# Both down projections of a two-block transformer kernel: six of eight half quarters by Strassen's seven products

## The chip, the cores and the metric

One NeuronCore of a Trainium2 chip runs the whole program. The metric is device time in microseconds (us) of that core, the median of three executions. The engines are TensorE (PE), VectorE (DVE), ScalarE (ACT), GpSimd (POOL) and SyncE (SP, which here only starts transfers).

## The reference

Two transformer blocks on 512 tokens of 1024 features, in float32. Each has mixers (convolution, sparse attention, cross attention; then a chunked linear recurrence and a latent attention) and ends in a feed forward. Only the feed forwards matter here:

```python
hf = _rmsnorm(h, norm_ffn_g[l]) @ w_ff1[l]            # 512x1024 @ 1024x4096
h = h + jnp.square(jax.nn.relu(hf)) @ w_ff2[l]        # 512x4096 @ 4096x1024
...
y = jnp.square(jax.nn.relu(m @ w_up[l])) @ w_down[l]
x = x + rmsnorm(y, norm_post_mlp[l])
```

## The kernel before, in words

Every float32 operand is split in two float32r parts, a rounded "hi" and the remainder "lo", and a product is three matmuls, hi by hi, lo by hi and hi by lo (L511 to L515). Activations lie feature by feature: 128 features on the partitions, 512 tokens along the row. A weight chunk is 1024 rows by 128 columns, 128x1024 in the memory, and gives one output of 128x512 with 8 x 3 = 24 matmuls (L524).

**The weight ring.** All chunks come in the order of their use through a ring of four slots. SP starts the transfer of chunk c when chunk c-4 is used up (L386 to L391). ACT rounds it to w_hi (L1218), POOL writes the remainder w_lo in place of the raw weights (L410), PE waits for w_lo_done. ACT keeps three chunks ahead.

**A feed forward** is four groups of 16 chunks. Eight "up" chunks (L829) give eight blocks of the hidden layer: DVE takes relu and the norm's scale (L2146), ACT squares (L1494) and rounds (L1496), DVE writes the remainder b_lo (L2149). Then eight "down" chunks multiply these eight blocks, and DVE adds each output to res (first block) or ffy (second), L2157. So 64 ups and 64 downs in all. The first block's feed forward is FF1 in the code, the second's FF2. A group works on a quarter of the 4096 hidden features; a half quarter is four up chunks and 512 hidden features.

**Around them.** Beside the first group of FF1 DVE computes the angles of the rotary embedding (`rotary`, L2186 to L2206, steps that wait for each other) and ACT their sines. FF2's first three chunks are computed in two halves of tokens while DVE, POOL and ACT still normalize the mixer's output (L1130 to L1161; post_scale L2510, post_split L2520, post_tree L2528 on DVE; post_add L485 on POOL; post_row on ACT). PE sums squares for a norm with a matmul by ones (`stat`), ACT takes the root (L1232), DVE the reciprocal (L1767, L2571).

Each engine executes its instructions in the order in which its block of the program issues them, and semaphores are the only order between engines. An engine that waits holds back all that is written behind the wait.

Of the kernel before, what the change touches and what calls it, by code (L numbers as in the profile page):

```python
# [20 lines left out]
ALU = mybir.AluOpType  # L21
# [29 lines left out]
FF_GROUPS = 4  # L51
# [10 lines left out]
          ("GL", 3), ("AO", 8), ("CO", 8), ("MX", 8), ("QX", 4), ("OX", 4), ("FF1", 64), ("CQ", 2), ("CKV", 1),  # L62
          ("KR", 1), ("QK", 4), ("UQ", 2), ("UKV", 1), ("OA", 1), ("VM", 4), ("OM", 3), ("WO", 8), ("FF2", 64)]
CH = {}
_n = 0
for _name, _count in STAGES:
# [5 lines left out]
        ("GL", 3), ("AO", 8), ("CO", 8), ("MX", 8), ("QX", 4), ("OX", 8), ("FF1", 64), ("CQ", 2), ("CKV", 1),  # L72
        ("KR", 1), ("QK", 4), ("UQ", 8), ("UKV", 8), ("OA", 1), ("VM", 4), ("OM", 3), ("WO", 11), ("FF2", 68)]
# [55 lines left out]
angles centred cn_hi_done cn_ready cn_scaled conv_done convact_ready cq_squared f_hi f_ready f_sq floors_done  # L129
gains_ready gate_step gated gates_done gates_late gates_turned gcols_done hg_hi hg_ready ki_split kr_moved  # L130
kv_keys_done kv_odd kv_values_done late_landed ln_added ln_hi ln_inv ln_root ln_scaled ln_silu ln_squared ln_sum
logits_ready mean2 mem_added mem_scaled mem_squared mix_added mix_hi mix_ready ml_conv ml_decay ml_den ml_diag
ml_floor ml_gated ml_hi ml_inv ml_mrow ml_ones ml_out ml_ready ml_root ml_s ml_sT ml_saved ml_scaled ml_sq
ml_turned ml_var norm2 o_gated o_hi o_ready o_scaled o_turned ox_first pT_copied pT_ready p_inv p_ready p_scaled
pad_zeroed post_added post_first post_scaled post_summed pv_done q_moved q_roped q_zeroed qi_split qk_pad
qk_rows_zeroed qk_silu relu_ready res_sq res_sqg rope_done rope_q rope_step row_step rows_done rstd_ready
rt_cols rt_done rt_turned s_masked s_ready scales_ready score_added sines spread_done squares
squares_added ssq_added ssqg_added start_hi start_ready start_scaled stat_ready stat_root tap_done topk_done
topk_step uq_out vm_rows wi_copied wi_turned x2_done x2_gained y_pool y_scaled y_written half_done half_rooted half_sums part_sq part_ssq qk_tanh post_tree post_sq first_w first_x first_hi first_lo
# [28 lines left out]
def program(nc, stream, xT, memT, cols_in, consts_in, pos_in, out):  # L168
    with ExitStack() as ctx:
# [80 lines left out]
        ff_f = at("ff_f", [P, 2, T], TMP0 + 4096)  # L250
# [68 lines left out]
        x_landed = [sem(f"x_landed{i}") for i in range(RING)]  # L319
# [43 lines left out]
        def up_bank(s, g, o0, j):  # L363

            if s == 1 and g == 0 and j in (4, 5):
                return j + 2
            return (o0 + j) % RING
# [6 lines left out]
        def _(sp):  # L374
# [11 lines left out]
            with sp.Fori(1, CHUNKS // RING) as i:  # L386
                for j in range(RING):
                    sp.wait_ge(chunk_done, RING * i + j - (RING - 1))
                    sp.dma_start(w_raw[:, j, :],
                                 stream[bass.ds(RING * i + j, 1), :, :].rearrange("o p n -> (o p) n")  # L390
                                 ).then_inc(raw_landed[j], 16)  # L391
            vector_adds = [j for j in range(KB) if j not in POOL_ADDS]
# [12 lines left out]
        def _(pool):  # L405
# [6 lines left out]

            last = CH["FF2"] // RING
# [7 lines left out]
            pool.wait_ge(sems["first_hi"], 1)  # L421
            first_remainder(0, sems["first_lo"])
# [3 lines left out]
            with pool.Fori(1, CH["CQ"] // RING) as i:  # L426
                for j in range(RING):
                    remainder(RING * i + j, j)
            pool.wait_ge(sems["pv_done"], 4 * MLA_G)
# [65 lines left out]
            with pool.Fori(last + 1, CHUNKS // RING) as i:  # L495
                for j in range(RING):
                    remainder(RING * i + j, j)
# [9 lines left out]
        def _(pe):  # L507
# [147 lines left out]
            def first_values():  # L655
                for kk in range(2):
                    w = slice(kk * T, (kk + 1) * T)
                    pe.wait_ge(w_hi_done if kk else sems["first_hi"], 1)
# [3 lines left out]
                for kk in range(2):  # L662
                    w = slice(kk * T, (kk + 1) * T)
                    pe.wait_ge(w_lo_done if kk else sems["first_lo"], 1)
# [2125 lines left out]
```

## Time and profile before

| | |
|---|---|
| median of three executions | 1583.17 us (1582.39 to 1584.31) |
| span of the profiled execution, first to last instruction | 1579.8 us |
| PE busy | 1545.0 us, 98% of the span, 7370 matmuls |
| POOL, DVE, ACT busy | 653.6, 838.6, 652.4 us |
| share of the chain that ended last | PE 90%, DVE 4%, ACT 2%, POOL 1% |

No time of its own is listed for the profiled execution beside its span; the median of the executions lies 3.4 us above that span. A busy share is the share of the span in which an engine has an instruction under way. Matmuls overlap, so their pace is read from the distance of their starts, not from their durations.

### The profile page before, as it was taken

How to read it: one execution, taken by the hardware profiler on the slowest of the kernel's cores; microseconds unless marked ns; L12 is line 12 of the kernel's file. 1: busy time of each engine (PE TensorE's matmuls, PEld its weight loads, DVE VectorE, ACT ScalarE, POOL GpSimd, SP SyncE). 2: the span in 40 equal slices, each digit the busy share in tenths (PEclk: the TensorE clock that was granted, in tenths of full speed). 3: DMA queues.
4: the chain of work that ended last, by engine and by line, in shares of the span. 5: the costliest groups of instructions: out<-in, count | busy, mean ns of one | idle time of the engine just before them, and what ended most of it. 6: DMA issues, size and time to landing. Idle time of an engine off the chain costs nothing.

```text
span 1579.8 us, 21097 instructions
## 1 busy us (share of the span) xinstructions
PE 1545.0 (98%) x7370; PEld 1278.8 (81%) x7370; DVE 838.6 (53%) x1486; ACT 652.4 (41%) x1066; POOL 653.6 (41%) x299
## 2 busy tenths in 40 slices
PE   8999999999999999999999999999999999999997
PEld 6888888787788877888888888777778888888887
DVE  5689999877785446442112124877645612111125
ACT  6553333444552445523233244455754514232331
POOL 3454444323344433444444445442524544444442
PEclk9999999999999999999999999999999999999999
DMA  5332333222333322323333333221112333333332
GB/s 208 102 121 94 94 101 98 67 67 67 107 95 102 96 67 67 101 93 99 101 93 93 104 96 94 83 71 61 41 49 73 96 104 93 94 98 102 94 93 81
DMA packets 41412, 144.57 MB, mean 92 GB/s; under 512 B 4596, under 2 KB 6772, under 8 KB 41080
## 3 DMA queue, kind: packets, MB, share of 16 engines
q1 hardware_dynamic: 40320, 139.94, 28.7%
q10 hardware_dynamic: 1016, 3.62, 0.7%
q8 instruction: 48, 0.79, 0.2%
q14 instruction: 28, 0.23, 0.1%
HBM read 141.43 MB, written 2.11 MB: 91 GB/s over the span
## 4 chain that ended last, share of the span: by engine, by line
PE 90%; DVE 4%; issue 3%; ACT 2%; POOL 1%; DMA 0%; DVEq 0%; SPq 0%; POOLq 0%; ACTq 0%
PE bank L509 88%; PE bank L619 1%; POOL w_lo L410 1%; POOL res L485 1%; DVE cq_rstd L1767 0%; PE bank L1014 0%; DVE bias L1913 0%; ACT w_hi L1218 0%; DMA x_raw<-in_xT 0%; DMA w_raw<-in_stream 0%; ACT kT L1392 0%; DVE cn_lo L2261 0%; DVE gt L2284 0%; DVE ffy L2600 0%; ACT probs L1251 0%
## 5 line engine op out<-in xcount | busy, mean ns | idle before, releaser
L410 POOL TENSOR_TENSOR w_lo<-w_raw,w_hi 128x1024 fp32r<-128x1024 f32 x250 | 602.6, 2411 | 849.6 <-ACT w_hi L1218 849.2
L1218 ACT CAST w_hi<-w_raw 128x1024 fp32r<-128x1024 f32 x255 | 267.4, 1049 | 499.2 <-DMA w_raw<-in_stream 499.2
L509 PE MATMUL bank<-a_hi,w_hi 128*128 128x512 f32 (+1 forms) x1120 | 445.0, 397 | 3.1 <-DVE a_lo L2520 1.8
L509 PE MATMUL bank<-a_hi,w_lo 128*128 128x512 f32 (+1 forms) x1120 | 431.5, 385 | 0.0
L509 PE MATMUL bank<-a_lo,w_hi 128*128 128x512 f32 (+1 forms) x1120 | 431.2, 385 | 0.0
L509 PEld LDWEIGHTS bank<-a_hi,w_hi 128*128 128x128 f32 x1120 | 210.5, 188 | 50.9 <-issue 4.2
L509 PEld LDWEIGHTS bank<-a_lo,w_hi 128*128 128x128 f32 x1120 | 210.6, 188 | 45.6 <-issue 3.6
L509 PEld LDWEIGHTS bank<-a_hi,w_lo 128*128 128x128 f32 x1120 | 210.4, 188 | 42.3
L509 PE MATMUL bank<-b_hi,w_hi 128*128 128x512 f32 (+1 forms) x640 | 244.3, 382 | 0.0
L509 PE MATMUL bank<-b_hi,w_lo 128*128 128x512 f32 (+1 forms) x640 | 242.3, 379 | 0.0
L509 PE MATMUL bank<-b_lo,w_hi 128*128 128x512 f32 (+1 forms) x640 | 242.2, 378 | 0.0
L509 PEld LDWEIGHTS bank<-b_hi,w_hi 128*128 128x128 f32 x640 | 120.4, 188 | 22.8 <-issue 0.2
L509 PEld LDWEIGHTS bank<-b_lo,w_hi 128*128 128x128 f32 x640 | 120.4, 188 | 22.5 <-issue 0.2
L509 PEld LDWEIGHTS bank<-b_hi,w_lo 128*128 128x128 f32 x640 | 120.4, 188 | 22.5
L2146 DVE SCALAR_TENSOR_TENSOR ff_t<-bank,rstd 128x512 f32<-128x512 f32 x64 | 44.1, 689 | 148.5 <-PE bank L509 148.4
L2149 DVE TENSOR_TENSOR b_lo<-ff_f,b_hi 128x512 fp32r<-128x512 f32 x64 | 47.9, 748 | 86.8 <-ACT b_hi L1496 86.8
L1977 DVE SCALAR_TENSOR_TENSOR bank<-conv_in,cols,bank 128x512 f32<-128x512 f32 x114 | 82.3, 749 | 1.6
L2157 DVE TENSOR_TENSOR res<-bank,res 128x512 f32<-128x512 f32 x32 | 22.1, 691 | 109.0 <-PE bank L509 109.0
L1956 DVE SCALAR_TENSOR_TENSOR bank<-conv_in,cols,bank 128x512 f32<-128x512 f32 x116 | 76.5, 745 | 0.0
L1494 ACT ACTIVATE ff_f<-ff_t 128x512 f32<-128x512 f32 x64 | 40.5, 632 | 85.5 <-DVE ff_t L2146 85.5
L2157 DVE TENSOR_TENSOR ffy<-bank,ffy 128x512 f32<-128x512 f32 x20 | 13.8, 691 | 84.3 <-PE bank L509 84.3
L1260 ACT COPY probsT<-bank 128x256 f32<-128x256 f32 (+3 forms) x48 | 19.6, 409 | 58.0 <-PE bank L619 58.0
(355 smaller groups left out, 1961.3 us busy)
## 6 DMA issues: line engine op xcount, KB each, us to landing
w_raw<-in_stream SPq DMA_DIRECT2D x255, 512.0 KB, 3.5
res<-in_xT ACTq DMA_DIRECT2D x1, 2048.0 KB, 8.0
out_y<-y_out SPq DMA_DIRECT2D x16, 128.0 KB, 1.8
x_raw<-in_xT SPq DMA_DIRECT2D x3, 512.0 KB, 8.3
mem_raw<-in_memT SPq DMA_DIRECT2D x1, 1024.0 KB, 11.9
mrow<-m_rows ACTq DMA_DIRECT2D x4, 256.0 KB, 3.2
w_raw<-in_stream SPq DMA_DIRECT2D x2, 256.0 KB, 3.6
x_raw<-in_xT SPq DMA_DIRECT2D x2, 256.0 KB, 4.2
```

Source lines behind the costliest of these rows:

```text
L410: nc.gpsimd.tensor_tensor(w_lo[:, j, :], w_raw[:, j, :], w_hi[:, j, :].bitcast(F32), ALU.subtract).then_inc(w_lo_done, 1)
L485: nc.gpsimd.tensor_tensor(res[:, j, t], res[:, j, t], mixed[:, j, t], ALU.add).then_inc(sems["post_added"], 1)
L509: return nc.tensor.matmul(o, l, r, start=start, stop=stop)
L619: m = nc.tensor.transpose(turned_bank(U)[:, r], probs[:, U % 2, r], ident)
L1218: A.copy(w_hi[:, slot, :], w_raw[:, slot, :]).then_inc(w_hi_done, 1)
L1260: A.copy(probsT[:, U % 2, r], turned_bank(U)[:, r]).then_inc(sems["pT_copied"], 1)
L1494: A.activation(ff_f[:, j % 2, :], ff_t[:, j % 2, :], ACT.Square).then_inc(sems["f_sq"], 1)
L1956: V.scalar_tensor_tensor(out=blk(conv_io, e, 0, T) if last else acc, in0=u, scalar=w, in1=acc, op0=ALU.mult, op1=ALU.add).then_inc(sems["c ...
L1977: m = V.scalar_tensor_tensor(out=out, in0=u, scalar=w, in1=acc if start is None else start, op0=ALU.mult, op1=ALU.add)
L2146: V.scalar_tensor_tensor(out=ff_t[:, j % 2, :], in0=bank, scalar=0.0, in1=rstd[:, :], op0=ALU.max, op1=ALU.mult).then_inc(evac_dve, 1)
L2149: V.tensor_tensor(b_lo[:, j, :], ff_f[:, j % 2, :], b_hi[:, j, :].bitcast(F32), ALU.subtract).then_inc(sems["f_ready"], 1)
L2157: V.tensor_tensor(dst[:, i, :], bank, dst[:, i, :], ALU.add).then_inc(evac_dve, 1)
```

## The change

Hidden block and down weights of a half quarter are 512 tokens by 512 hidden features and 512 by 1024. Split into 2x2 blocks (tokens in halves, hidden blocks by even and odd, outputs in halves), the product takes eight block products, or seven by Strassen's method (in Winograd's form) with sums of blocks on both sides. Six half quarters of each feed forward go that way; the last quarter (8 ups, 8 downs) stays as it was. The hidden block is now the stationary operand, so the results lie token by token (ytok) and are turned back on PE in the last quarter, where DVE scales them by rstd squared (r2) and adds them.

Weights: the four blocks of a half quarter (L11, L21, L22, L12, each 128x1024) come by four transfers outside the ring into dn_raw. DVE makes four sums of them, ACT rounds seven (`top`), POOL writes seven remainders in place (`rest`). FF1 and FF2 have 40 ring chunks each in place of 64, and 24 blocks beside them.

```diff
+            def product(s, g, n, x, banks):
+                q = HALVES * s + g
+                pe.wait_ge(sems["apart_lo"], APART + PRODUCTS * q + n + 1)
+                for h in range(2):
...
+                    for p in range(2):
...
+                        mm(o, xh, wh, p == 0, False)
+                        mm(o, xh, wl, False, False)
+                        m = mm(o, xl, wh, False, p == 1)
+                    m.then_inc(sems["dn_done"], 1)
+            def ff_down(s, g):
+                last, evac = 4 * g + 2, evac_before(s, g)
...
+                pe.wait_ge(sems["b_ready"], b_at(s, last, 1))
+                product(s, g, M1, E1, (4, 5))
...
+                pe.wait_ge(sems["b_ready"], b_at(s, last, 2))
+                product(s, g, M5, T1, (6, 7))
...
+                product(s, g, M7, T3, (0, 1))
+                product(s, g, M6, T2, (2, 3))
+                pe.wait_ge(sems["dn_evac"], evac + 2 * (M7 + 1))
+                product(s, g, M4, T4, (0, 1))
...
+                product(s, g, M2, O1, (4, 5))
+                product(s, g, M3, O2, (6, 7))
+            def turn_block(s, i):
...
+                for tb in range(TB):
+                    m = nc.tensor.transpose(ps[4 + i % RING][:, tb * P:(tb + 1) * P],
+                                            ytok[:, tb, i * P:(i + 1) * P], ident)
```

POOL, in order of its queue (`remainder` is the ring's w_lo):

```diff
+            def rest(s, g, names=BY_ORDER):      # L11 S1 S3 S2 L22 L12 S4
+                for name in names:
+                    pool.wait_ge(sems["apart_hi"], APART + PRODUCTS * q + n + 1)
+                    if name in ("L11", "S1"):
+                        pool.wait_ge(sems["dn_sum"], 4 * q + 3)
+                    elif name == "L22":
+                        pool.wait_ge(sems["dn_sum"], 4 * q + 2)
+                    elif name in ("S2", "L12"):
+                        pool.wait_ge(sems["dn_sum"], 4 * q + 4)
+                    nc.gpsimd.tensor_tensor(dn_rest[:, n, :], dn_raw[:, n, :], dn_top[n].bitcast(F32), ALU.subtract
...
+            for g in range(HALVES):
+                rest(0, g)
+                for c in range(CH["FF1"] + 4 * (g + 1), CH["FF1"] + 4 * (g + 2)):
+                    remainder(c, c % RING)
...
+            remainder(CH["FF2"] + 4, 0)
+            rest(1, 0, ("L11",))
+            remainder(CH["FF2"] + 5, 1)
+            rest(1, 0, BY_ORDER[1:])
+            remainder(CH["FF2"] + 6, 2)
+            remainder(CH["FF2"] + 7, 3)
+            rest(1, 1)
+            for g in range(2, HALVES):
+                for c in range(CH["FF2"] + 4 * g, CH["FF2"] + 4 * g + 4):
+                    remainder(c, c % RING)
+                rest(1, g)
```

ACT, one half quarter:

```diff
+            def ff_half(s, g):
+                j = 4 * g
+                square_up(s, j)
+                even_casts(s, j)          # E1, T1: 256 columns each
+                top(s, g, "S2", "L22")
+                square_up(s, j + 1)
+                odd_casts(s, j + 1)       # T3: 256; T2 and T4: 512; O1 and O2: 512
+                top(s, g, "L12", "S4")
+                square_up(s, j + 2)
+                even_casts(s, j + 2)
+                square_up(s, j + 3)
+                odd_casts(s, j + 3)
+                round_to(ff_chunk_at(s, j + 7) - AHEAD)
...
+            top(0, 0, "L11", "S1", "S3")
+            root(3, rstd[:, :], STAT, 1.0 / D)
+            ff_half(0, 0)
+            for g in range(1, HALVES):
+                top(0, g, "L11", "S1", "S3")
+                ff_half(0, g)
```

DVE, one half quarter (even_block: one sum of 256 columns; even_lo: two remainders of 256; odd_block: three sums of 256, remainders of 256, 512 and 512; left_sum: 1024 columns; take_products: fourteen results of 128x512 from PSUM):

```diff
+                evict_up(s, j)
+                even_block(s, j)
+                even_lo(s, j)
+                left_sum(s, g, "S4")
+                evict_up(s, j + 1)
+                odd_block(s, j + 1)
+                evict_up(s, j + 2)
+                even_block(s, j + 2)
+                even_lo(s, j + 2)
+                evict_up(s, j + 3)
+                odd_block(s, j + 3)
+                take_products(s, g)
...
+            for g in range(1, HALVES):
+                left_sum(0, g, "S3")
+                left_sum(0, g, "S1")
+                left_sum(0, g, "S2")
+                ff_half(0, g)
+            ff_whole(0)                   # seven sums of 128x1024, then r2
+            ff_last(0, res, last_ff1, rotary)
```

In FF2 the first two half quarters are ordered by hand (DVE after post_tree):

```diff
+            evict_up(1, 0)
+            evict_up(1, 1)
+            even_block(1, 0)
+            even_lo(1, 0)
+            evict_up(1, 2)
+            evict_up(1, 3)
+            left_sum(1, 0, "S3")
+            left_sum(1, 0, "S1")
+            even_block(1, 2)
+            even_lo(1, 2)
+            odd_block(1, 1)
+            left_sum(1, 0, "S2")
+            odd_block(1, 3)
+            left_sum(1, 0, "S4")
+            evict_up(1, 4)
+            evict_up(1, 5)
```

ACT's order there is round_to(FF2+1), square_up 0 and 1, even_casts 0, round_to(FF2+2), square_up 2 and 3, even_casts 2, root(9), top S1 and S3, odd_casts 1, top S2, odd_casts 3, top L22, L12, S4. PE computes chunks 3, 4 and 5, then ff_down(1, 0), chunks 6 and 7, ff_down(1, 1). The rotary work of DVE and ACT moves from FF1's first downs to its last ups (`if j == 4`, `if 4 < j < 7`, counted from 0 in the last quarter).

## Rows read from the trace of the kernel before

**Rows 1.** The page, sections 1 and 4: busy time, and the chain by engine and line

```profile
PE 1545.0 (98%) x7370; PEld 1278.8 (81%) x7370; DVE 838.6 (53%) x1486; ACT 652.4 (41%) x1066; POOL 653.6 (41%) x299
...
PE bank L509 88%; PE bank L619 1%; POOL w_lo L410 1%; POOL res L485 1%; DVE cq_rstd L1767 0%; PE bank L1014 0%; DVE bias L1913 0%; ACT w_hi L1218 0%; DMA x_raw<-in_xT 0%; DMA w_raw<-in_stream 0%; ACT kT L1392 0%; DVE cn_lo L2261 0%; DVE gt L2284 0%; DVE ffy L2600 0%; ACT probs L1251 0%
```

**Rows 2.** DVE in order of time, a down of FF1: start, us, instruction, idle before

```profile
709.84 0.69 DVE L2157 TENSOR_TENSOR res<-bank,res 128x512 f32<-128x512 f32 x1 [4.75 <-PE bank L509]
```

**Rows 3.** PE in order of time: four transposes between 512-column matmuls

```profile
999.73 0.60 PE L866 MATMUL bank<-consts,ssq 128*128 128x128 f32 x4
1000.08 0.47 PE L509 MATMUL bank<-a_hi,w_hi 128*128 128x512 f32 x1
1000.40 0.39 PE L509 MATMUL bank<-a_lo,w_hi 128*128 128x512 f32 x1
```

**Rows 4.** By source line: duration ns min/median/max, first and last start, forms

```profile
L410 POOL TENSOR_TENSOR w_lo<-w_raw,w_hi x250: 2358/2400/2854, 20.8 to 1549.7; 128x1024 fp32r<-128x1024 f32 x125
L1218 ACT CAST w_hi<-w_raw x255: 1029/1050/1066, 8.6 to 1548.5; 128x1024 fp32r<-128x1024 f32 x128
L1494 ACT ACTIVATE ff_f<-ff_t x64: 632/632/635, 644.6 to 1523.7; 128x512 f32<-128x512 f32 x64
L1842 DVE TENSOR_TENSOR w_lo<-w_raw,w_hi x5: 1217/1226/1566, 9.7 to 1217.0; 128x1024 fp32r<-128x1024 f32 x5
L2149 DVE TENSOR_TENSOR b_lo<-ff_f,b_hi x64: 691/692/1306, 645.9 to 1525.0; 128x512 fp32r<-128x512 f32 x64
L2154 DVE COPY ffy<-bank x8: 690/692/692, 1267.3 to 1305.4; 128x512 f32<-128x512 f32 x8
```

**Rows 5.** DVE and ACT in order of time: instructions of 256 columns

```profile
1196.90 0.43 DVE L2494 TENSOR_TENSOR ssq<-ssq,sq 128x256 f32<-128x256 f32 x1 [0.48 <-ACT sq L1691]
...
1196.45 0.42 ACT L1691 ACTIVATE sq<-mixed 128x256 f32<-128x256 f32 x1 [1.97 <-DVE mixed L2485]
```

**Rows 6.** POOL, then DVE, in order of time from 1253 to 1259 us

```profile
1253.29 2.41 POOL L410 TENSOR_TENSOR w_lo<-w_raw,w_hi 128x1024 fp32r<-128x1024 f32 x1 [8.79 <-ACT w_hi L1218]
1255.94 2.57 POOL L410 TENSOR_TENSOR w_lo<-w_raw,w_hi 128x1024 fp32r<-128x1024 f32 x1 [0.24 <-ACT w_hi L1218]
...
1254.94 1.31 DVE L2149 TENSOR_TENSOR b_lo<-ff_f,b_hi 128x512 fp32r<-128x512 f32 x1 [1.35 <-ACT b_hi L1496]
```

**Rows 7.** The same two engines at 20 us (DVE's four merged)

```profile
20.75 2.73 POOL L410 TENSOR_TENSOR w_lo<-w_raw,w_hi 128x1024 fp32r<-128x1024 f32 x1 [12.92 <-ACT w_hi L1218]
23.70 2.59 POOL L410 TENSOR_TENSOR w_lo<-w_raw,w_hi 128x1024 fp32r<-128x1024 f32 x1 [0.21 <-ACT w_hi L1218]
...
19.75 7.09 DVE L1831 TENSOR_TENSOR x_sq<-x_sq 128x512 f32<-128x512 f32 x4
```

**Rows 8.** The page, section 6: transfers of a weight chunk, KB, us to landing

```profile
w_raw<-in_stream SPq DMA_DIRECT2D x255, 512.0 KB, 3.5
```

**Rows 9.** Start of FF1: its first matmul on PE, DVE's last sum before it

```profile
627.13 0.39 PE L509 MATMUL bank<-a_hi,w_hi 128*128 128x512 f32 x1
...
634.37 0.68 DVE L2089 TENSOR_TENSOR ssq<-ssq,sq 128x512 f32<-128x512 f32 x1
```

**Rows 10.** Start of FF2: PE's chunk 3, DVE's last tree, ACT's cast of chunk 4

```profile
1232.87 0.40 PE L509 MATMUL bank<-a_hi,w_hi 128*128 128x512 f32 x1
...
1230.06 4.85 DVE L2528 TENSOR_TENSOR mixed<-mixed 128x1024 f32<-128x1024 f32 x6
...
1236.13 1.05 ACT L1218 CAST w_hi<-w_raw 128x1024 fp32r<-128x1024 f32 x1 [6.20 <-DMA w_raw<-in_stream]
```

**Rows 11.** PE's last dense matmul; window: busy by engine, granted clock, DMA, GB/s

```profile
1568.76 0.28 PE L509 MATMUL bank<-b_hi,w_lo 128*128 128x256 f32 x1
...
1570.00:1575.00 5.00, 1.54 (x10) 1.26 (x10) 2.99 (x10) 0.26 (x1) 1.56 (x2) 0.78 0.04 13
```

**Rows 12.** PE's first matmuls, eight of 512 columns

```profile
5.82 3.88 PE L509 MATMUL bank<-w_hi,xu_hi 128*128 128x512 f32 x8 [5.82 <-ACT xu_hi L1297]
9.54 2.01 PE L509 MATMUL bank<-w_lo,xu_hi 128*128 128x512 f32 x8
```

More of the change, by code:

```diff
@@ L50, with done_before, evac_before, added_at @@
 MLA_V = 64
-FF_GROUPS = 4
+HALVES = 6
+UPS = 4 * HALVES
+BY_ORDER = ("L11", "S1", "S3", "S2", "L22", "L12", "S4")
+SLOT = {name: n for n, name in enumerate(BY_ORDER)}
+LEFT = ("L11", "L21", "L22", "L12")
+SLOT["L21"] = SLOT["S1"]
+M1, M5, M7, M6, M4, M2, M3 = range(7)
+E1, O1, O2, T1, T3, T2, T4 = range(7)
+PRODUCTS = 7
+PARTS_DONE = 2 * PRODUCTS
+WHOLE_STEPS = 7
+def done_before(s, g):
+    return (PARTS_DONE * HALVES + KB) * s + PARTS_DONE * g
+def evac_before(s, g):
+    return (PARTS_DONE * HALVES + WHOLE_STEPS + 1 + 2 * KB) * s + PARTS_DONE * g
+def added_at(s, i):
+    return evac_before(s, HALVES) + WHOLE_STEPS + 1 + (2 - s) * (i + 1)
+def evens_first(s, g):
+    return s == 1 and g < 2
+def b_before(s, g):
+    return (10 * HALVES + KB) * s + 10 * g
+def b_at(s, j, n):
+    g, p = j // 4, j // 2 % 2
+    if evens_first(s, g):
+        return b_before(s, g) + (2 * p + n if n <= 2 else 2 + 3 * p + n)
+    return b_before(s, g) + 5 * p + n
+def sum_at(s, j, n):
+    g, p = j // 4, j // 2 % 2
+    if evens_first(s, g):
+        return 8 * (HALVES * s + g) + (p + n if n == 1 else 1 + 3 * p + n)
+    return 8 * (HALVES * s + g) + 4 * p + n
 RING = 4
@@ L318, in program @@
         mem_landed = sem("mem_landed")
[L319 removed]
+        x_landed = [sem(f"x{i}_and_{name}_landed") for i, name in enumerate(LEFT)]
+        dn_landed, LANDED_X, APART = x_landed, 16, 1
         x_again = sem("x_landed_again")
@@ L854, in norm_ffn, with ff_up @@
-            def norm_ffn():
-                stat(3, STAT, [(sems["ssq_added"], 2 * KB, ssq[:, :])])
-            feed_forward("FF1", 0, 1, norm_ffn, 1)
+            def ff_up(s, j, ks=range(KB), ready=None, base=0):
+                c, o = ff_chunk_at(s, j), ff_out_at(s, j)
+                g = j // 4
+                if g > 0 and ks[0] == 0 and up_bank(s, j) < RING:
+                    pe.wait_ge(sems["dn_evac"], evac_before(s, min(g, HALVES) - 1) + 2 * (M4 + 1))
+                chunk(c, c % RING, o if up_bank(s, j) < RING else None, up_bank(s, j), a_hi, a_lo, T, ready, base, ks=ks)
@@ new lines, in ff_last @@
+            def ff_last(s, downs):
+                for j in range(KB):
+                    ff_up(s, UPS + j)
+                    if 2 <= j < 6:
+                        turn_block(s, 2 * j - 4)
+                        turn_block(s, 2 * j - 3)
+                for j in range(UPS + KB, UPS + KB + downs):
+                    c, o = ff_chunk_at(s, j), ff_out_at(s, j)
+                    chunk(c, c % RING, o, o % RING, b_hi, b_lo, T, sems["b_ready"] if j == UPS + KB else None, b_before(s, HALVES))
@@ new lines, in take @@
+            def take(s, g, n, dst, banks):
+                for h in range(2):
+                    dve.wait_ge(sems["dn_done"], done_before(s, g) + 2 * n + h + 1)
+                    bank = ps[banks[h]][:, :]
+                    if g == 0:
+                        V.tensor_copy(dst[h], bank).then_inc(sems["dn_evac"], 1)
+                    else:
+                        dve.wait_ge(sems["dn_evac"], evac_before(s, g - 1) + 2 * n + h + 1)
+                        V.tensor_tensor(dst[h], bank, dst[h], ALU.add).then_inc(sems["dn_evac"], 1)
```

558 lines of the change are left out of this document (417 added, 141 removed).

## The prediction

> **What bounds the kernel now.** I read the page first. PE is busy for 1545.0 of 1579.8 us, and its matmuls are 88% of the chain that ended last; no other engine passes 53% [rows 1]. Next comes the order of time inside a feed forward: DVE takes one output of 24 matmuls in 0.69 us after an idle 4.75 us that PE ends [rows 2]. So a chunk is 5.44 us of PE, a matmul of 512 columns 0.227 us, and each matmul taken from PE is worth that as long as nothing else comes late. Then I looked at what the other engines' instructions cost alone and beside each other, since the change loads DVE and POOL.
>
> **What goes.** A half quarter now has 4 ups and 4 downs, 8 x 24 matmuls. The seven products have 12 each: 84 in place of 96. Twelve halves save 144 x 0.227 = 32.6 us.
>
> **Transposes.** 16 blocks of four. Four transposes move the second matmul behind them from 0.227 to 0.67 us after their start [rows 3], 0.44 us a block: 16 x 0.44 = 7.0 us. The Trainium skill, "TensorE: Matmul & The Clock Gate", Part 4: PE-mode transpose, has about 275 ns for one transpose in a kernel; by it the 64 would cost 17.6 us and the sum would be 10.6 us higher. The trace has such durations too, but shows them overlapping, so I go by the starts.
>
> **Prices of the added work.** DVE with 1024 columns 1.22 us, with 512 columns 0.69 (from PSUM too), ACT's cast of 1024 columns 1.05 and square 0.63, POOL's remainder 2.40 [rows 4]; 256 columns 0.43 on DVE, 0.42 on ACT [rows 5]. A relu without the norm's scale has no row; I take the 0.69 of a PSUM read (it could be 0.43, the row of half its columns, or 0.75).
>
> **What decides: DVE and POOL hold each other up.** A b_lo of 0.69 us took 1.31 where POOL's remainder ran: POOL ended at 1255.70, b_lo 0.55 us later, at 1256.25. POOL's next, which had started at 1255.94, ended 2.26 us after that [rows 6]. At 20 us DVE had four instructions to do in a row and needed 7.09 us for them, 2.4 us of which is their own; working back from the ends, POOL got in behind the second and again behind the third [rows 7]. So two-input DVE work in SBUF and POOL's remainders exclude each other, and when both queue up they take turns: DVE pays the rest of a POOL instruction (up to 2.3 us) for each of its own. Before, POOL ran one remainder per 5.44 us, and this hid. Now a half quarter has 7 + 4 remainders (26.4 us) and 22 such DVE instructions.
>
> **A half in the steady state**, from the start u of its ups (the last product of the half before ends). DVE takes that product until u+0.8, then S3, S1, S2 at 1.24 each: u+4.5. Only now may POOL start L11. From here, with s = time since S2:
> - POOL L11, S1, S3, and between them DVE's three short ones (t1, E1 lo, T1 lo; 0.3 us each when admitted): s = 8.1. DVE's S4 sum: 9.3.
> - POOL's S2 runs (2.4) while DVE evicts the second block and ACT squares it: 11.7. T3 sum 0.3, POOL's L22 2.26, T2 sum 0.3, T4 sum 0.45: 15.0.
> - ACT casts T2/T4 and O1/O2 (1.1), then tops L12 and S4 (1.9), and only then squares the third block (0.63): s = 18.6. POOL's L12 has begun at 17.2 and ends at 19.6; t1 of the third block 19.9; POOL's S4 has the turn, 22.1; E1 lo 22.4.
> M1 waits for that E1 lo: u+26.97. The four ups end at u+21.76. **PE waits 5.2 us.** All later products are covered: T3 lo is ready 3 us after M1 begins, M7 needs it after 5.4, and DVE's takes keep up with 2.72 us a product. The half takes 21.76+5.2+19.04 = 46.0 us where it took 43.5.
> Transfers land in 3.5 us [rows 8]; L22's slot is free 5.4 us before u, L12's 2.7 before, so they are no wait, nor are SP's ring transfers queued behind them.
>
> **First half of FF1.** Ups begin at 627.13, DVE is free at 635.0 [rows 9]. S3, S1, S2 with one POOL remainder between end at 640.8; ACT's root and its table load follow two tops, so the first square is at about 643.6. The same chain gives M1 at 663.8; the ups end at 649.6: 14.2 us.
> **FF1's last quarter.** ff_whole, seven sums of 1.22 us, delays the evictions but four banks cover it. DVE then has evict, remainder, two turned blocks (3.6 to 4.3 us) per up, and at the sixth and seventh up also seven rotary steps, 3.9 us bare and about 6 with POOL's turns. It runs about 8 us late, and the first down lacks its last block for 5.5 us. The cover these steps had, DVE's idle 4.75 us per down, is gone.
> **Start of FF2.** Chunk 3 begins at 1232.87, DVE's tree ends at 1234.9, ACT casts chunk 4 from 1236.13 [rows 10]. DVE reaches the S2 sum only behind two odd or even blocks that wait for ACT (squares, root, tops S1 and S3, casts): at 1252.8. POOL's rest of L11 waits for it, and **behind that on POOL stands chunk 5's remainder**: ready at 1257.7, PE came at 1244.5. 13.2 us, and 1.0 more for bank 7 before M5. Second half: S2 sum at 1295.8, L11 at 1298.3 against 1294.2 (4.1), then 0.4 for T3 and 2.3 for rest S2, whose sum S4 came late by two turns: 6.8. Third half: POOL is still at four ring remainders when DVE wants its sums, S2 4.2 us later than in the steady state: 9.4.
>
> **The sum.** Waits of FF1: 14.2 + 5 x 5.2 + 5.5 = 45.7. Of FF2: 13.2+1.0 + 6.8 + 9.4 + 3 x 5.2 = 46.0. Together 91.7 - 32.6 + 7.0 = +66.1 us.
> **The clock** comes on top. The dense matmuls ended at 1568.9 us; in the window 1570 to 1575 the mean grant is 0.78, so 2.4 GHz was granted for 2.8 us of it, to 1572.8, and 1.2 GHz then: 3.9 us after, with a few small matmuls between [rows 11]. At the start eight matmuls took 3.72 us where eight take 1.8 at full clock [rows 12]: 1.9 us for a fall. Three long waits surely pay it (5.7); of the nine of 5.2 to 5.5 us, between none and all (17.1): half, 8.5, since one fall beside small matmuls can't say more. +14. The skill's same page, "Why this matters for your kernels", advises to leave no idle gaps between bursts of matmuls, since they bring the low clock back; by it all twelve waits pay, and the time would be 1672. The trace has no such gap between dense matmuls.
> Against the profiled span of 1579.8 that gives 1660; the median is 3.4 above that span: **1663 us**, bounds 1649 (no falls) to 1680 (all falls and longer waits); evictions at the ends of their range move each half by under 0.3 us.
>
> **Rivals.**
> - *DVE keeps the turn in a run of short sums.* For: each of its instructions waits in the queue ready. Against: rows 7. T1 lo and T2 sum each save 2.3 us, a steady half waits 0.7. Waits: 8 x 0.7, 9.7 at FF1, 11 + 5 + 5 in FF2, 5 rotary: 41, clock 4: 1583.2-25.6+45 = 1603.
> - *The exclusion doesn't reach these instructions* (smaller, or hidden in gaps). Then every steady wait is gone; what stays is chunk 5's place on POOL's queue (11), the second half's late sum (4), the rotary (4), one fall (2): 1583.2-25.6+21 = 1579, faster. Its place is the wait of M1; it decides once POOL's seven rests need under 17 us from S2 with DVE's work between (22.4 by my walk).
> - *PE stays the bound everywhere*, by the same and with ACT's and POOL's start-up work landing early: 1583.2-25.6 = 1557.6. Against it: POOL can't have chunk 5 before DVE's S2 sum. That the matmuls don't go can't be: the count is fixed in the code.
>
> **Chances.** Forecast (1640 to 1690) 0.73, first rival 0.12, second 0.09, third 0.06. Slower by over 0.2% (about what a measurement of this kernel can tell): 0.73+0.12 = 0.85, less 0.01; the second lies at -0.3%: 0.07 faster, 0.02 same; with the third and a hundredth more for same: faster 0.13, same 0.03, slower 0.84. Range: the forecast's case and nearly all of the first rival, 1600 to 1690.
>
> **What would show it.** Right: PE waits before M1 of each half, ended by DVE's f7_lo (E1), about 5 us each; before chunk 5 of FF2 a wait ended by POOL, over 10 us; DVE sums of 256 columns with a mean well over 1 us; POOL near two thirds busy in the halves; starts of products 0.227 us apart; PE clock below 1 in slices. Wrong: DVE's 256-column sums at 0.43 us, or halves of 41 us, or waits ended by transfers.

## The result, and the profile after

The changed kernel takes **1678.15 us** (1674.69 to 1679.59), the kernel before, run beside it, 1583.74: a ratio of 1.059, 95% interval 1.058 to 1.061, 94.4 us slower. The forecast was 1663 us. The spans of the profiled executions differ by 98.0 us (1677.8 against 1579.8); the sums below go by these two.

The page of the changed kernel, its sections 1, 2 (the clock's line) and 5:

```profile
span 1677.8 us, 20806 instructions
PE 1553.3 (93%) x7290; PEld 1279.1 (76%) x7290; DVE 1196.9 (71%) x1862; ACT 704.2 (42%) x1174; POOL 745.6 (44%) x335
...
PEclk9999999999999998999999999999999898999998
...
L655 PE MATMUL bank<-dn_first,f_hi 128*128 128x512 f32 x192 | 84.8, 442 | 71.2 <-issue 66.1
```

Against [rows 1]: 80 instructions fewer on PE (144 matmuls less, 64 transposes more), yet PE is busy 8 us longer, because part of them ran at the lower clock. DVE gained 358 us, POOL 92. PE's idle time grew from 34.8 to 124.5 us. The last line says where: of 71.2 us before matmuls with `dn_first` (rounded weights, L11 for M1), 66.1 are marked "issue", which means that the view found no releaser. The line alone doesn't say what PE waited for. The waits of PE, grouped (us in total, times, longest):

```profile
PE bank L655 <- issue: 66.3, 11, 13.2
PE bank L655 <- POOL w_lo L524: 10.8, 2, 9.8
...
PE bank L655 <- DVE b_lo L2578: 6.0, 2, 4.9
PE bank L655 <- POOL dn_rest L538: 5.2, 2, 4.2
```

and PE in order of time: the first matmul of M1 in FF1's first four halves, then FF2's start, where the first line is chunk 5's and the two others M1's in the second and third halves:

```profile
663.40 0.77 PE L655 MATMUL bank<-dn_first,f_hi 128*128 128x512 f32 x1 [13.16 <-issue]
715.13 0.77 PE L655 MATMUL bank<-dn_first,f_hi 128*128 128x512 f32 x1 [8.43 <-issue]
763.23 0.77 PE L655 MATMUL bank<-dn_first,f_hi 128*128 128x512 f32 x1 [5.06 <-issue]
811.21 0.77 PE L655 MATMUL bank<-dn_first,f_hi 128*128 128x512 f32 x1 [5.05 <-issue]
...
1310.51 0.79 PE L655 MATMUL bank<-a_hi,w_hi 128*128 128x512 f32 x1 [9.75 <-POOL w_lo L524]
...
1353.26 0.47 PE L655 MATMUL bank<-dn_first,f_hi 128*128 128x512 f32 x1 [4.21 <-POOL dn_rest L538]
...
1406.26 0.77 PE L655 MATMUL bank<-dn_first,f_hi 128*128 128x512 f32 x1 [9.09 <-issue]
```

Two more of FF1 and three of FF2 are like the third and fourth. For what M1 waits DVE's order of time tells, from the half's first block on:

```profile
791.27 0.48 DVE L2460 TENSOR_TENSOR comb<-ff_f 128x256 f32<-128x256 f32 x1 [0.70 <-ACT ff_f L1703]
791.71 2.58 DVE L2466 TENSOR_TENSOR f_lo<-ff_f,f_hi 128x256 fp32r<-128x256 f32 x1
794.22 2.61 DVE L2469 TENSOR_TENSOR f_lo<-comb,f_hi 128x256 fp32r<-128x256 f32 x1
...
807.43 1.20 DVE L2460 TENSOR_TENSOR comb<-ff_f 128x256 f32<-128x256 f32 x1 [1.05 <-ACT ff_f L1703]
808.55 2.56 DVE L2466 TENSOR_TENSOR f_lo<-ff_f,f_hi 128x256 fp32r<-128x256 f32 x1
```

and POOL's beside it (the first line is three rests merged):

```profile
789.07 7.48 POOL L538 TENSOR_TENSOR dn_rest<-dn_raw,dn_first 128x1024 fp32r<-128x1024 f32 x3 [11.38 <-DVE dn_raw L2438]
798.11 2.40 POOL L538 TENSOR_TENSOR dn_rest<-dn_raw,dn_first 128x1024 fp32r<-128x1024 f32 x1 [1.57 <-DVE dn_raw L2444]
800.47 2.58 POOL L538 TENSOR_TENSOR dn_rest<-dn_raw,dn_second 128x1024 fp32r<-128x1024 f32 x1
806.00 4.83 POOL L538 TENSOR_TENSOR dn_rest<-dn_raw,dn_second 128x1024 fp32r<-128x1024 f32 x2 [2.95 <-ACT dn_second L1697]
```

E1's remainder of the half's third block (L2466) ends at 811.11 and M1 begins at 811.21: that is the "issue". An operation of 256 columns, 0.43 us alone [rows 5], takes 2.56 to 2.61 us here where a rest of POOL began just before it, and 1.20 where the rest was already half done. Between two such operations one rest passes, never two. The view by source line has the spread (ns min/median/max; first and last start):

```profile
L2466 DVE TENSOR_TENSOR f_lo<-ff_f,f_hi x24: 414/2564/2628, 646.2 to 1549.0; 128x256 fp32r<-128x256 f32 x24
```

Set beside POOL's timeline, 20 of the 24 take 2.56 to 2.63 us, and a rest had begun 0.24 to 0.28 us before each of them. The other four, of FF2's first two halves, take 0.41 or 0.42, and no rest runs beside them.

### The profile page after: what moved, and what is told of

Same layout as the page of the kernel before. It is cut to its first block and busy times, and to the rows that moved or that the text cites. A ratio compares the mean times of both kernels' runs of the same rounds, so it can differ in the third digit from the quotient of the medians.

```text
span 1677.8 us, 20806 instructions
## 1 busy us (share of the span) xinstructions
PE 1553.3 (93%) x7290; PEld 1279.1 (76%) x7290; DVE 1196.9 (71%) x1862; ACT 704.2 (42%) x1174; POOL 745.6 (44%) x335
## 5 line engine op out<-in xcount | busy, mean ns | idle before, releaser
L524 POOL TENSOR_TENSOR w_lo<-w_raw,w_hi 128x1024 fp32r<-128x1024 f32 x202 | 488.8, 2429 | 668.6 <-ACT w_hi L1427 668.5
L655 PEld LDWEIGHTS bank<-a_hi,w_lo 128*128 128x128 f32 x1120 | 211.1, 188 | 42.7
L538 POOL TENSOR_TENSOR dn_rest<-dn_raw,dn_first 128x1024 fp32r<-128x1024 f32 x48 | 118.2, 2483 | 153.2 <-DVE dn_raw L2438 131.2
L655 PE MATMUL bank<-dn_first,f_hi 128*128 128x512 f32 x192 | 84.8, 442 | 71.2 <-issue 66.1
L655 PE MATMUL bank<-dn_rest,f_hi 128*128 128x512 f32 x336 | 139.5, 415 | 0.0
L655 PE MATMUL bank<-b_hi,w_hi 128*128 128x512 f32 (+1 forms) x256 | 95.9, 374 | 6.0 <-DVE b_lo L2578 6.0
L538 POOL TENSOR_TENSOR dn_rest<-dn_raw,dn_second 128x1024 fp32r<-128x1024 f32 x36 | 88.3, 2470 | 29.5 <-ACT dn_second L1697 29.5
L655 PE MATMUL bank<-b_hi,w_lo 128*128 128x512 f32 (+1 forms) x256 | 93.4, 365 | 0.0
L655 PE MATMUL bank<-b_lo,w_hi 128*128 128x512 f32 (+1 forms) x256 | 93.3, 365 | 0.0
L655 PE MATMUL bank<-dn_first,f_lo 128*128 128x512 f32 x192 | 82.6, 430 | 0.0
L655 PEld LDWEIGHTS bank<-dn_rest,f_hi 128*128 128x128 f32 x336 | 68.3, 203 | 14.5
```

The lines of the kernel that those rows point to most:

```text
L524: nc.gpsimd.tensor_tensor(w_lo[:, j, :], w_raw[:, j, :], w_hi[:, j, :].bitcast(F32), ALU.subtract).then_inc(w_lo_done, 1)
L538: nc.gpsimd.tensor_tensor(dn_rest[:, n, :], dn_raw[:, n, :], dn_top[n].bitcast(F32), ALU.subtract).then_inc(sems["apart_lo"], 1)
L655: return nc.tensor.matmul(o, l, r, start=start, stop=stop)
```

## The experiments

My theory after this reading: PE's waits before M1 come from **turns** that DVE and POOL take at a shared access to SBUF (the on-chip memory that both read), two waits in FF2's start from the **order of POOL's queue**, two at FF1's end from the **rotary steps**, and each wait of some 5 us costs about 2.3 us more by **TensorE's clock**. Ratios are against the kernel before on the same chip, with 95% intervals; line numbers shift by one to seven between kernels.

### POOL's rests read nothing

```diff
-                    nc.gpsimd.tensor_tensor(dn_rest[:, n, :], dn_raw[:, n, :], dn_top[n].bitcast(F32), ALU.subtract
-                                            ).then_inc(sems["apart_lo"], 1)
+                    nc.gpsimd.memset(dn_rest[:, n, :].bitcast(F32), 0.0).then_inc(sems["blank"], 1)
+                    pool.wait_ge(sems["blank"], PRODUCTS * q + BY_ORDER.index(name) + 1)
+                    nc.gpsimd.memset(dn_rest[:, n, :].bitcast(F32), 0.0).then_inc(sems["apart_lo"], 1)
```

> POOL's seven remainders of a half quarter are left out: in their place two memsets of 1024 columns each write zeros there (so the hi-by-lo share of the products is missing). POOL then still takes time for each of the seven, but reads nothing from SBUF. Theory (DVE and POOL exclude each other and take turns): the waits of PE before the first product M1, 5.06 us in the steady state, fall under 1 us, DVE's E1 remainders (median 2.56 us now) go back to 0.43, the first half of FF1 waits under 4 us where it waited 13.2; with the clock's falls gone too the time is 1590 to 1610. The wait before FF2's chunk 5 stays at 7 us or more, since it is an order on POOL's queue. Rival (the order of ACT's and DVE's own queues sets M1, POOL's port doesn't matter): waits before M1 stay at 4 us or more and the time is over 1660.

Measured: **1593.72 us**, ratio 1.006 (1.004 to 1.009), as the theory had it. The same line of DVE, and the waits that PE has left:

```profile
L2467 DVE TENSOR_TENSOR f_lo<-ff_f,f_hi x24: 412/426/426, 646.1 to 1467.0; 128x256 fp32r<-128x256 f32 x24
```

```profile
PE bank L656 <- POOL w_lo L524: 10.6, 2, 9.6
...
PE bank L656 <- DVE b_lo L2579: 5.3, 2, 4.9
PE bank L656 <- POOL dn_rest L540: 3.8, 1, 3.8
PE bank L656 <- issue: 3.7, 1, 3.7
```

All 24 are at 0.41 to 0.43 us, and no steady half waits for M1, while DVE's queue, ACT's and the matmuls are as in the changed kernel. The edit also makes a rest shorter (1.91 us for two memsets of 0.956 where it was 2.36), so by this run alone some of the gain could be POOL's; the run with ACT's casts in another order, below, keeps all of the reads and settles that. What stays, the 9.6 of chunk 5, the 4.9 of FF1's first down, the 3.8 of FF2's second half and the 3.7 of FF1's first, doesn't need POOL's reads.

### PE kept busy before M1

```diff
+                    for _ in range(24):
+                        mm(ps[4][:, :], a_hi[:, 0, 0:P], a_hi[:, 0, :])
                 pe.wait_ge(sems["b_ready"], b_at(s, last, 1))
                 product(s, g, M1, E1, (4, 5))
```

> 24 matmuls of 512 columns, whose result is overwritten, stand before M1 of each half but the first of each feed forward, so PE works through 5.44 us of the wait. Theory (each wait also costs about 2.2 us of low clock behind it): M1 comes 0.4 us later than before, but the halves take 46.3 us where they take 47.8 to 48.1, the granted clock stays at full in them, and the time is about 1660. Rival (the falls cost nothing that counts, the 2 us a half are something else): 1680 to 1684.

Measured: **1663.84 us**, 1.051 (1.048 to 1.053). M1 to M1 in steady halves takes 46.26 us (763.99 to 810.23, to 856.50) where it took 47.98 and 47.88. The waits are as long as before, only filled with matmuls of no use (5.45 us for 5.06), and 46.26 is 40.8 and 5.45: nothing of the clock is left in such a half, where it had been 2.0 to 2.1 us. The time is 14 us shorter, as expected.

### The order of ACT's last two casts, and POOL's last three rests held back

First the casts alone:

```diff
                 odd_casts(s, j + 1)
-                top(s, g, "L12", "S4")
                 square_up(s, j + 2)
                 even_casts(s, j + 2)
+                top(s, g, "L12", "S4")
```

> One move on ACT's queue: the tops of L12 and S4 come after the casts of the third block instead of before its square. All work stays. Theory: the square comes only 0.4 us earlier, but POOL has no remainder ready to take the turn when t1 and E1 lo of the third block come, so M1's wait falls from 5.06 to about 1.9 us, the eight steady ones together by 25 us, and the clock's falls mostly go: 1637. Rival (ACT's order alone): each wait 0.4 to 1.5 us shorter, 1665 to 1675. Rival (only the number of instructions on the port counts): no change.

Measured: **1642.9 us**, 1.038 (1.035 to 1.040). The waits of 5.06 before M1 became 1.87 to 1.88, and the two of 8.43 and 9.09 became 5.26 and 5.94; in two halves a new one of 1.3 stands before M7. The third block of a half, DVE and then POOL:

```profile
841.89 0.42 DVE L2460 TENSOR_TENSOR comb<-ff_f 128x256 f32<-128x256 f32 x1 [0.70 <-ACT ff_f L1703]
842.33 0.43 DVE L2466 TENSOR_TENSOR f_lo<-ff_f,f_hi 128x256 fp32r<-128x256 f32 x1
```

```profile
843.78 4.93 POOL L538 TENSOR_TENSOR dn_rest<-dn_raw,dn_second 128x1024 fp32r<-128x1024 f32 x2 [5.91 <-ACT dn_second L1697]
```

This is the plainest proof of the turns, since all of the work and all of POOL's reads are there. ACT's square starts only 0.36 us earlier behind DVE's relu than in the changed kernel (0.72 us after the relu's start, 1.08 before). The other 2.9 us are DVE's two short operations, 1.20 and 2.56 us when two rests stood beside them [807.43 and 808.55 above], 0.42 and 0.43 now that POOL's rests come behind them. Together they are, to 0.1 us, what M1's wait lost. The rival of ACT's order alone (1665 to 1675 us) is out.

Then POOL's rests of L22, L12 and S4 behind T3's remainder of the fourth block as well:

```diff
+            def rest_held(s, g):
+                rest(s, g, BY_ORDER[:4])
+                pool.wait_ge(sems["b_ready"], b_at(s, 4 * g + 2, 3))
+                rest(s, g, BY_ORDER[4:])
```

> As the ACT order alone, and POOL also holds its remainders of L22, L12 and S4 back until T3 lo of the fourth block is done, so that they run while DVE reads PSUM. All work stays. Theory: steady waits before M1 under 1 us, no wait before M4, M2, M3, POOL's ring remainders end about 2 us into the next ups; time 1605 to 1620. If POOL's work and not the turns was the limit, new waits before M4 to M3 or before the next ups take their place and the time stays over 1650.

Measured: **1636.11 us**, 1.033 (1.031 to 1.035), a miss: 16 us above what was expected at most. The steady halves no longer wait for M1, but before M4, 2.2 us each:

```profile
761.68 0.80 PE L660 MATMUL bank<-dn_second,f_hi 128*128 128x512 f32 x1 [2.21 <-DVE ytok L2505]
```

because a part of the turns had been moved, onto the remainders of 512 columns behind the hold (DVE, then POOL):

```profile
797.34 2.69 DVE L2491 TENSOR_TENSOR f_lo<-comb,f_hi 128x512 fp32r<-128x512 f32 x1 [0.35 <-ACT f_hi L1724]
799.96 2.90 DVE L2494 TENSOR_TENSOR f_lo<-ff_f,f_hi 128x512 fp32r<-128x512 f32 x1
```

```profile
797.07 8.03 POOL L538 TENSOR_TENSOR dn_rest<-dn_raw,dn_second 128x1024 fp32r<-128x1024 f32 x3 [9.32 <-DVE f_lo L2488]
```

DVE then takes the products' results 4 us late, and M4 waits for M7's bank. I had not looked at who needs DVE next behind the hold. Even so a half is shorter, 43.3 us where no fall of the clock follows the wait, against 44.5 with the casts' order alone.

### The two orders at the quarters' ends

Chunk 5's remainder ahead of the rest of L11:

```diff
             remainder(CH["FF2"] + 4, 0)
-            rest(1, 0, ("L11",))
             remainder(CH["FF2"] + 5, 1)
+            rest(1, 0, ("L11",))
```

> One line moved: on POOL the remainder of FF2's chunk 5 now stands ahead of the half's rest of L11. Theory (chunk 5 waits only because its remainder is queued behind L11's, which waits for DVE's S2 sum): the 9.75 us before chunk 5 go, M1 of that half waits instead for L11's chain, some 2 to 4 us; with the clock of one wait that comes to 1668 to 1672 us. Rival (chunk 5 is late for ACT's cast or its transfer): no change from 1678.

Measured: **1676.33 us**, 1.059 (1.057 to 1.061), no different from the changed kernel: a miss. Chunk 5 no longer waits, so its place on the queue was the cause of that wait (the 0.9 us before chunk 4 stay), but two others, before M1 and before M5, stand where one stood:

```profile
1310.18 0.76 PE L655 MATMUL bank<-dn_first,f_hi 128*128 128x512 f32 x1 [3.63 <-POOL dn_rest L538]
1318.95 0.80 PE L655 MATMUL bank<-dn_first,f_hi 128*128 128x512 f32 x1 [4.19 <-DVE ff_t L2452]
```

7.8 us in place of 9.75, and each with a fall of the clock. The second is M5, whose bank DVE has yet to empty of the up before (the 1.0 us that the prediction has for it, now in the open). All of this stands behind one DVE chain, the S2 sum and then the odd block, with POOL's turns in it.

The rotary steps back beside the downs (DVE's part of the edit; ACT's two sines move with them):

```diff
-                if j == 4:
+                if j == KB:
...
-                if 4 < j < 7:
-                    dst, turn_off, off = ((sinT, 0.0, 0.0), (cosT, 0.25, float(np.pi / 2)))[j - 5]
-                    n = 2 + 6 * (j - 5)
+                if KB < j < KB + 3:
+                    dst, turn_off, off = ((sinT, 0.0, 0.0), (cosT, 0.25, float(np.pi / 2)))[j - KB - 1]
+                    n = 2 + 6 * (j - KB - 1)
```

> The rotary steps on DVE and ACT's two sines go back from FF1's ups (the fifth to seventh) to its third to fifth downs from last. Theory: DVE is no longer behind in the last quarter, the waits of 1.16 and 4.88 us before the last two blocks of FF1's first down go: 1668 to 1672 us. Rival (DVE is late there for its turned blocks alone, two of them per up): most of the 6 us stays, 1675 or more.

Measured: **1672.96 us** (two runs, 1668.16 and 1677.76), 1.057 (1.053 to 1.061). Both waits of FF1's first down (1.16 and 4.88) are gone, which the rival did not have; a new one of 2.20 us stands ahead of the mixer, ended by DVE's a_lo. The two times are too far apart to size the gain (mean granted clock 0.974 in the shorter, 0.966 in the other, whose trace this is).

### All of these together, with the hold lengthened

The hold of `rest_held` at `b_at(s, 4 * g + 2, 5)`, so behind the fourth block's last remainder.

> e4's edit (ACT's tops of L12 and S4 behind the third block's casts, POOL's rests of L22, L12 and S4 held back), with the hold lengthened from the fourth block's E1 remainder to its O remainders, so that none of DVE's remainders of the half meets POOL's last three rests; and with the edits of e5 and e6. Theory of turns: both e4's gains stay and its 2.2 us before M4 go too, as well as chunk 5's and the rotary's wait; what is left are the first halves' waits (7.6, 3.1 us): 1595 to 1605 us. Rival (the 2.2 us before M4 come from DVE's work alone): about 1620.

Measured: **1616.79 us**, 1.022 (1.020 to 1.024), 12 us above what the theory had at most. The time is near the rival's 1620, but not for its reason: the waits before M4 are gone, so DVE's work alone didn't make them. 1.7 to 1.8 us before M1 are back in most steady halves, which take 42.7 to 42.9 us. One more hold, so that DVE's first two remainders meet no rest:

```diff
-                rest(s, g, BY_ORDER[:4])
+                rest(s, g, BY_ORDER[:1])
+                pool.wait_ge(sems["b_ready"], b_at(s, 4 * g, 2))
+                rest(s, g, BY_ORDER[1:4])
```

> e8's kernel with one more hold: POOL rests L11, then waits for T1's remainder of the half's first block, and only then rests S1 and S3. Theory of turns: DVE's two remainders there (2.6 us each in e8, 0.43 alone) no longer pay, DVE is 3 to 4 us earlier, and the last 1.7 to 1.8 us before M1 go, half of the first halves' too: 1597 to 1607 us. Rival (the shared access is full, 39.7 us of the 40.8 of a half: 11 remainders of 2.36 and DVE's 13.7, so what one hold gives the next wait takes): 1612 to 1620.

Measured: **1615.12 us**, 1.020 (1.018 to 1.022): the rival's number, and not clearly less than without the second hold. DVE in order of time:

```profile
775.82 0.41 DVE L2473 TENSOR_TENSOR f_lo<-ff_f,f_hi 128x256 fp32r<-128x256 f32 x1
776.37 0.42 DVE L2476 TENSOR_TENSOR f_lo<-comb,f_hi 128x256 fp32r<-128x256 f32 x1
...
780.40 2.62 DVE L2486 TENSOR_TENSOR comb<-ff_f,comb 128x256 f32<-128x256 f32 x1
783.05 2.51 DVE L2488 TENSOR_TENSOR comb<-ff_f,comb 128x256 f32<-128x256 f32 x1
```

The two remainders are short, as the hold wants, and the two sums of the next block are long in their place. M1 waits 1.63. By an estimate from these durations the access is nearly full: in a half POOL needs 11 x 2.38 = 26.2 us of it, DVE four sums of 1.22, fourteen operations of 256 columns at 0.42 and four of 512 at 0.69, 13.5 together; that is 39.7 of the 40.8 us in which PE does the half's matmuls (4 x 5.44 + 84 x 0.227). The orders did give back most of the turns' price: a steady half takes 42.7 us here, 47.9 in the changed kernel. The last 1.9 us I put down to the full access; that no order could win them too is not shown.

### Both: no reads, and the two orders

> e1's edit (each POOL rest replaced by two memsets, which read nothing; the products' share of high part by rest of the second matrix is left out) with the edits of e5 and e6. Theory: the removed matmuls are worth their 25.6 us when nothing else is late; what is left are short waits in the first halves and before M1 in the second half: 1565 to 1578 us, below the kernel before. Rival (the clock or a hidden cost of the products takes it anyway): no less than 1583.

Measured: **1584.35 us** (1577.75 to 1585.3), ratio 1.000 (0.9985 to 1.0013): no difference, where 5 to 18 us of gain were expected. The steady halves take 40.8 us (696.61 to 737.41 to 778.21), the full gain of the removed matmuls, and little else is late.

Against the profiled 1579.8: -32.6 and +7.0, 15.0 us of waits that the kernel before has not (3.59, 0.98, 3.19, 3.79, 2.18, 1.25), together -10.6. The span is 1582.6, so 13.4 more. The granted clock was low six times before the tail, in a window of one of them (us, PE busy, clock, DMA share, GB/s):

```profile
1048.00:1051.00 3.00, 3.00 (x9) 0.50 0.02 5
```

Six falls at 2.3 us would be 13.8. Added up from the granted clock itself it is less: PE works 22.5 us at half clock before the tail, which costs 11.2. Two of the six falls lie in the mixer, which the change does not touch, and where the kernel before has nearly the same short waits (1.38 us for ogate, 1.82 here) and no fall; a third lies in FF2's first chunk, behind the wait of 1.25. So the rival that the clock takes it had a part of the truth. The ten executions bear it out: three took 1577.8 to 1579.2 us, at a mean granted clock of 0.994, the other seven 1583.7 to 1585.3, at 0.989 or 0.990.

### What a gap costs by itself

The kernel **before**, with twelve gaps in dense matmuls; the second run has GAP = 2:

```diff
+GAPS = (9, 12, 14)
+GAP = 7
...
+                        if j in GAPS:
+                            pe.wait_ge(sems["pad_zeroed"], gap_at(s, g, j, GAP))
                         ff_chunk(g, j, sems["f_ready"] if j == KB else None, g * KB + 32 * s)
...
+                        if not isinstance(g, int) and j + 1 in GAPS:
+                            for n in range(GAP):
+                                if n > 0:
+                                    dve.wait_ge(sems["pad_zeroed"], gap_at(s, g, j + 1, n))
+                                V.memset(ps[6][:, :], 0.0).then_inc(sems["pad_zeroed"], 1)
```

> The kernel before (not the changed one), with twelve gaps put into PE's dense matmuls in the middle quarters of the feed forwards: in front of the second, fifth and seventh down PE waits until DVE has taken the down before and filled an unused PSUM bank seven times, one after the other. Nothing else is late by it. It measures what a gap of about 5 us costs besides its own length. As the mis-sized term of the changed kernel's sum has it (35 us of clock in place of 14, with 14 waits of 4 to 13 us), a gap costs 2 to 3 us more than it lasts: with gaps of w us the time is 1583 + 12 x (w + 2.5), 1673 at w = 5. If falls of the clock are not it, and the 21 us are another loss of the changed kernel (its matmuls, its transposes), the time is 1583 + 12 x w to 12 x (w + 1).

> The same with two fillings in place of seven, gaps of 1.5 to 2.5 us. The changed kernel's waits of 1 us mostly show no fall of the granted clock and those of 3 us do, so I expect some of the twelve to fall: 1583 + 12 x w plus 0 to 20 us. If every gap pays alike, it is 12 x 2.5 = 30 us on top of the gaps.

Measured: **1684.65 us** with the long gaps, **1626.64** with the short ones. PE in order of time around one long gap, and the granted clock in windows there:

```profile
771.00 0.79 PE L517 MATMUL bank<-b_hi,w_hi 128*128 128x512 f32 x1 [5.63 <-DVE bank L2172]
771.58 0.63 PE L517 MATMUL bank<-b_lo,w_hi 128*128 128x512 f32 x1
772.01 0.63 PE L517 MATMUL bank<-b_hi,w_lo 128*128 128x512 f32 x1
...
776.09 0.40 PE L517 MATMUL bank<-b_hi,w_hi 128*128 128x512 f32 x1
```

```profile
768.50:769.00 0.50, 0.00 (x0) 1.00 0.06 25
769.00:770.00 1.00, 0.00 (x0) 0.50 0.00 0
...
775.00:776.00 1.00, 1.00 (x4) 0.58 0.00 0
```

The clock goes to 1.2 GHz (0.50) inside the gap, and the next eleven matmuls start 0.43 us apart in place of 0.227. The long gaps sum to 68.3 us; the kernel is 102.3 us longer, so 34.0 us are beside their length, one more fall in the mixer included: **2.6 us for each of the 13 falls**. In one group of downs, with three gaps (759.76 to 828.11, less the 43.52 without gaps and the 16.89 of the gaps), it is 2.65. All twelve show the fall. Of the twelve short ones (2.3 to 2.45 us, 27.8 in all) six do. The execution with the trace (1624.47 us) is 42.1 us longer than the kernel before, 14.3 beside the gaps, or 2.0 for each of seven falls, one of them again in the mixer; in a stretch of three short gaps with one fall the trace has 2.4. The other execution took 1628.81 us at a lower mean clock (0.988 against 0.990) and has no trace.

## Why the prediction was right

The likeliest case came true at its place and in its sign. Point by point, with the numbers of the changed kernel:

- **What goes, and the transposes:** 80 instructions fewer, as counted. Ups with two blocks of transposes beside them begin 6.34 us apart (951.06 to 957.40), 0.90 more than 5.44: 0.45 a block, where 0.44 was taken. The durations' reading, 17.6 us for the 64, is refuted.

```profile
951.06 0.48 PE L655 MATMUL bank<-a_hi,w_hi 128*128 128x512 f32 x1
957.40 0.47 PE L655 MATMUL bank<-a_hi,w_hi 128*128 128x512 f32 x1
```

- **Steady halves:** 5.06 us before M1, seven times, 5.2 forecast for eight. The walk through the three queues, turn by turn, was right to 0.15 us, and the run in which POOL reads nothing and the one with the casts' order show its cause. A relu without the norm's scale took 0.68 us, where 0.69 was taken.
- **First half of FF1:** 13.16 for 14.2. **Its second half:** 8.43 for 5.2, missed. The step that failed is that this half was taken as a steady one: ahead of its sums DVE has the reciprocal of the norm's root to do, 3.34 us, which is the whole difference, and which the prediction has no term for. POOL had ended its ring remainders at 677.85 us and stood idle for 15.1:

```profile
685.59 3.34 DVE L2050 RECIPROCAL rstd<-rstd 128x512 f32<-128x512 f32 x1
```

- **FF2's third half:** 9.09 for 9.4. POOL's four ring remainders (1371.12 to 1381.58) met two of DVE's sums, 3.27 and 3.24 us for 1.22, as the prediction had it:

```profile
1376.06 3.27 DVE L2429 TENSOR_TENSOR dn_raw<-dn_raw 128x1024 f32<-128x1024 f32 x1
```

- **FF1's first down:** 1.16 and 4.88, 6.04 for 5.5. The late rotary steps are the cause: put back, both waits are gone.
- **Chunk 5:** 9.75 for 13.2, with 1.05 before chunk 4 that was not forecast. POOL's queue shows the order that made it, the rest of L11 idle until DVE's S2 sum and chunk 5's remainder behind it:

```profile
1305.58 2.40 POOL L538 TENSOR_TENSOR dn_rest<-dn_raw,dn_first 128x1024 fp32r<-128x1024 f32 x1 [11.51 <-DVE dn_raw L2438]
1307.94 2.52 POOL L524 TENSOR_TENSOR w_lo<-w_raw,w_hi 128x1024 fp32r<-128x1024 f32 x1
```

- **Second half of FF2:** 4.21 and 0.95, 5.2 for 6.8. The 4.2 us stand in every run that does all of the work but the one whose filler matmuls cover a part; no experiment was made for them.
- **The waits together** are 88.1 us, 91.7 forecast.
- **The clock is the term that was mis-sized.** 98.0 + 32.6 - 7.0 - 88.1 leaves 35.5 us, where 14 was taken. The step that failed is "half of nine" at 1.9 us a fall, and with it the list of twelve waits: all 13 waits over 4 us brought the clock down (the 13th is the 4.21 of FF2's second half, which the list leaves out), and so did all twelve gaps of 5.6 us put into the kernel before; and two falls lie in the mixer, which had no term. Added up from the granted clock, PE works 62.2 us at half clock before the tail, which costs 31.1 us, about 2.1 for each of the 15 falls. So most of the miss is their number, 15 where seven or eight were priced. Some 4 us of the 35.5 are not the clock's by this sum; the tail behind the last product is 0.9 us longer, and for the rest I have no row. The Trainium skill ("TensorE: Matmul & The Clock Gate", Why this matters for your kernels), by whose rule all waits pay and which the prediction priced at 1672 us, agrees with these traces in that: none of the 13 was without a fall. The 1672 us were still low, since they leave out the three falls more and price each at the 1.9 us of the kernel's first matmuls [rows 12].

The miss of 15.2 us is +21.5 of clock, -3.6 of waits, and -3.0 because the median lies 0.3 us above the profiled span, not 3.4, which leaves 0.3 of rounding. (An execution takes some 1.8 us longer than its own span wherever both are on record; the profiled one after was the longest of its four, and the one before must have been a short one.) The first rival (DVE keeps the turn in a run of short sums) is refuted by the two long remainders at 791.71 and 794.22 with a rest between: the second is T1's, which should have been short. The second (the exclusion doesn't reach these instructions) needed 0.43 us beside a rest; in the changed kernel the 256-column operations last that long only where none runs. The third would need the steady half at 40.8 us, which only the runs without reads have, and a start without late work, which none has.

What stays open: why PE's short waits in the mixer bring the clock down in one kernel and not in another; and whether a version that does all of the work can be faster than the kernel before. None of those tried was (the best is 2.0% slower). But in that one a steady half takes 42.7 us, less than the 43.5 before: what it has over lies where the feed forwards start, in waits of 8.2 and 2.9 us in FF1's first two halves and of 3.6, 5.8, 4.2 and 3.6 in FF2's first three, 28 us together, and in the clock's falls behind them. Nothing but chunk 5's order was tried on these.

## What to carry to other kernels

Count what a change takes from the bound engine, and then what it puts on the engines beside it, by what they share: 5.44 us of PE per chunk hid one POOL remainder and one DVE operation, 40.8 us of PE per half did not hide 39.7 us of work on one access, because who comes second there pays up to a whole instruction of the other. Moving such work so that the two don't meet pays (61 to 63 us of the 94 came back, all of the work kept), but a piece of the wait turns up elsewhere (before M1, then before M4, then before M1 again); look each time at what stands behind the moved piece. Price a wait of the matmul engine at its length plus the slow matmuls after it, here 1.5 to 3.1 us for each wait over 4 us, 2.1 in the mean, by the granted clock. Look also for single long instructions ahead of a chain: one reciprocal of 3.34 us made a half 3.4 us later than its neighbours.

## What the runs showed of the hardware that I had not expected

- What the clock takes hardly grows with the wait: M1 to M1 is 51.73 us after the wait of 13.16, 40.8 and 8.43 of it matmuls and the next wait, 2.5 the clock's, near the 1.9 to 2.5 of the halves behind a wait of 5.06. Gaps of 2.3 us brought it down in six of twelve places, and I see no difference between the places. The wait of FF1's second half is 3.06 us with the first hold and shows no fall, 3.07 with the longer one and shows one.
- In its turn an operation of 256 columns lasts nearly as long as one of 512 (2.6 us against 2.7 to 2.9): what it pays is POOL's instruction, not its own length. The Trainium skill ("SBUF — State Buffer", SBUF: two separate sides) has DVE with two SBUF inputs and a GpSimd operation that reads SBUF exclude each other for the whole instruction; these durations agree, and so does the run without reads. When both had work queued up, they came here each in turn. POOL pays less: three rests with two of DVE's operations between them took 7.48 us, 2.49 each, where two ring remainders without any took 4.72 (in the run with the rests held), 2.36 each.
- DVE's operations with one input in PSUM (where PE writes its results) are outside of it. With the rests held, four of them took 2.47 us in all while POOL was at its third rest (797.07 to 805.10):

```profile
802.78 2.47 DVE L2505 TENSOR_TENSOR a<-bank,a 128x512 f32<-128x512 f32 x4
```
